# GLA half chunks laid between the MLA attention blocks, and rotated keys on 128 rows, in a two-layer streaming encoder step

## The chip, the cores and the metric

One Trainium2 chip, one of its cores. The metric is the device time of one execution in microseconds (us), from the program's start to its end. The kernel computes everything in one launch. All arithmetic of the parts below is in float32; a float32 matmul stands in the trace as two records.

## The reference, cut to what matters

The step has two layers on 304 new rows: 16 meta tokens and 256 prompt tokens (group i), and 32 sample tokens (group ii) with a past of 272 cached rows. Layer 0 mixes by two head groups beside each other, whose outputs are joined and projected; each layer then has a layer norm, a mixture of 64 experts, and a second norm. The change lies within the mixer of layer 0:

```python
lg = log_sigmoid(a @ gla_w_g2 + gla_b_g) / 16
o_gla, s_gla = gla_recurrence(q * 64 ** -0.5, k, v, lg, s0)      # 4 heads, chunks of 64 tokens
o_gla = rms_norm(o_gla, gla_norm_g) * silu(r)
...
def step(s, inp):                                                # one GLA chunk
    b = jnp.cumsum(gc, axis=2)
    o_inter = einsum('bhtd,bhdv->bhtv', qc * exp(b), s)          # what the state gives
    att = einsum('bhtd,bhsd,bhtsd->bhts', qc, kc, decay)
    o = o_inter + einsum('bhts,bhsv->bhtv', att, vc)
    s = exp(b_last)[..., None] * s + einsum('bhsd,bhsv->bhdv', kc * exp(b_last - b), vc)
    return s, o
...
s = (einsum('bhqc,bkc->bhqk', q_lat, k_lat) + einsum('bhqr,bkr->bhqk', q_rope, k_rope)) * MLA_SCALE
p = softmax(where(k_chunk <= q_chunk, s, NEG_INF))               # 8 heads
o_lat = einsum('bhqk,bkc->bhqc', p, k_lat)
...
out = concatenate([o_gla, o_mla], axis=-1) @ w_out0
```

A GLA chunk needs the state that the chunk before left. MLA and GLA don't depend on each other until the output projection.

## The kernel before, in words

Tokens lie in three tiles of 128, 128 and 64 columns (the last holds 16 prompt tokens, 32 sample tokens and zeros between). Five engines run programs of their own and wait on semaphores. PSUM has eight banks, and `Banks` gives them out in one fixed order: `bank_uses()` lists every use of a bank in the order in which TensorE issues it, use number i takes bank i modulo 8, `open` makes TensorE wait until the use eight places earlier has been emptied, `full` makes a reader wait for its filling, `copied` waits for a particular use's emptying. So the list sets not only what comes when, but also who waits for whom.

After the input projections and the transposes (until about 102 us) the mixer goes through these stages:

- **Level products** (`level_products(t)`, L1005). For tile t and each of four heads, the causal products within a chunk, by six levels and the diagonal, as small 64-row matmuls into one bank ("att", t, h). VectorE masks the bank (L1621) and sums the levels (L1625) into `att`, in `sum_levels(t)`.
- **Absorbed queries** ("ql", h, L1032): one matmul for each of eight MLA heads; **rotated queries** ("qrT", i, L749): 24 transposes. ScalarE copies both out (L1261).
- **GLA chunks** (`chunk_out(c)`). There are six: four of 64 prompt tokens, one of the last 16 (number 4) and the sample's 32 (number 5). Each has two halves j of two heads. A half takes two banks: ("o", c, j) with the queries on the state (L1018) and the level sums on the values (L1022), which ScalarE copies to `og` (L1261), and ("u", c, j), keys on values (L1025), which VectorE adds to the decayed state in two operations (L1637, `update_state`). A chunk of the prompt waits until the state of the one before has been added.
- The order before was, tile by tile: level products, then absorbed or rotated queries, then the tile's chunks, by `CHUNKS_BY_TILE = [[0], [1], [5, 2, 3, 4]]`. Behind them VectorE made the sums of squares of `og` (L1490, L1652), ScalarE the reciprocal root (L1269, L1270), and the norm (`norm_out`, L1490) was laid into attention steps 1, 3 and 5 on VectorE.
- **Attention** (19 blocks, `attention_blocks()`): for each of eight heads a block of queries 0 to 127 on 144 keys and one of queries 128 to 255 on 272 keys, so even blocks have 144 keys and odd ones 272; block 16 has the 16 tail queries of all heads on 272 keys, and 17 and 18 the sample's queries of four heads each on 320 keys (L765 with `skv_t`, `skr_t`). TensorE's step i issues the scores of block i (latent keys on 128 rows, then rotated keys on 32 rows, L765), the transposes of the probabilities of block i-2 (L749) and the weighted sum of block i-3 (L765, 128-key pieces, the last one 16 or 64 keys). VectorE's step m normalises block m (L1684, L1493), then does the mask, maximum and negation of scores m+2 (L1670, L1672, L1493) and copies the sum of block m-2 (L1497). ScalarE's step m has the exponential of block m+1 (L1375) and the copies of the transposes of block m (L1385, L1386).
- Then the transposes of `og` (L749), the value matmuls of MLA ("om", L1101) and the output projection (L765, 64 records).

SP issues the load of the output weights (4 MB) when the last level product has filled its bank (L639), and the shared expert's weights when the norm is done (L552, L555). POOL stores the GLA states when the last state additions are done (L713).

## Time and profile before

| | us |
|---|---|
| time, median of 3 runs (lowest, highest) | 1508.03 (1506.62, 1508.96) |
| the profiled execution: its time | 1507.37 |
| the profiled execution: its span, first to last instruction | 1505.6 |
| mean granted TensorE clock | 0.942 |
| TensorE busy (PE) | 1435.9, 95% of the span |
| VectorE busy (DVE) | 634.3, 42% |
| ScalarE busy (ACT) | 348.5, 23% |
| first level product | 102.05 |
| first score matmul's load | 159.42 |
| output projection starts | 249.28 |

Two lines of the page's second part show the span in 40 slices of 37.6 us; PE is TensorE's busy share and PEclk its granted clock, in tenths:

```profile
PE   6999899899999999999999978999999999999994
PEclk9996557899999999999999989999999999999997
```

The fourth to the seventh slice (113 to 263 us) are those with a granted clock of 6, 5, 5 and 7 tenths. A granted clock of 1.00 is TensorE's 2.4 GHz level, 0.50 its 1.2 GHz level. The chain of work that ended last lies to 93% on TensorE. In the rows below PE is a matmul, PEld a weight load; a line's last bracket is the engine's idle time before it and who ended it, and "issue" stands for time in which it waited for nothing that the profile shows. A matmul's duration contains its way through the array, so the distance of two starts tells what one costs.

### The profile page before, as it was taken

The numbers are of one execution on the slowest core, as the hardware profiler recorded it, in microseconds if no ns is written. First come the engines' busy times: TensorE is split into PE (matmuls) and PEld (weight loads), VectorE is DVE, ScalarE is ACT, GpSimd is POOL, SyncE is SP. The second block draws the span as 40 slices with busy tenths as digits, with TensorE's granted clock in tenths as the row PEclk, the third lists the DMA queues.
The fourth block names the chain that finished last, engine by engine and source line by source line (L and its number), as shares of the span: only waits on it lengthen the run. The fifth ranks groups of instructions, "written<-read, shape, count | busy, mean of one in ns | idle before, by whom it ended". The sixth has DMA issues, their size and how long they took to land.

```text
span 1505.6 us, 17800 instructions
## 1 busy us (share of the span) xinstructions
PE 1435.9 (95%) x6519; PEld 753.0 (50%) x6519; DVE 634.3 (42%) x1267; ACT 348.5 (23%) x722; POOL 49.1 (3%) x77
## 2 busy tenths in 40 slices
PE   6999899899999999999999978999999999999994
PEld 4565465464454454455445465545445445444542
DVE  0554542562433343344334368334334333433436
ACT  1441321221221222122122213122212122222211
POOL 5200100100000000000000020000000000000000
PEclk9996557899999999999999989999999999999997
DMA  9102020176998999899899842599989989998970
GB/s 297 62 6 113 8 91 0 65 300 270 375 391 349 410 387 393 366 394 392 347 412 391 349 151 103 205 372 391 390 364 395 392 348 410 390 390 364 395 305 31
DMA packets 63623, 435.21 MB, mean 289 GB/s; under 512 B 4324, under 2 KB 6436, under 8 KB 13537
## 3 DMA queue, kind: packets, MB, share of 16 engines
q1 hardware_dynamic: 60800, 427.08, 71.0%
q0 software_dynamic: 2784, 7.62, 1.6%
q8 instruction: 24, 0.39, 0.1%
q14 instruction: 15, 0.12, 0.0%
HBM read 432.93 MB, written 1.76 MB: 289 GB/s over the span
## 4 chain that ended last, share of the span: by engine, by line
PE 93%; DVE 4%; issue 1%; ACT 1%; DMA 0%; SPq 0%; DVEq 0%
PE bank L849 30%; PE bank L765 25%; PE bank L797 15%; PE bank L791 12%; PE bank L749 4%; PE bank L859 1%; PE bank L919 1%; DVE sb_x L1519 1%; PE bank L1025 1%; PE bank L906 1%; DVE sb_x L1515 1%; PE bank L1022 1%; DVE sb_ln_st L1511 1%; PE bank L1018 1%; DMA sb_x<-in_x_sample_dram 0%
## 5 line engine op out<-in xcount | busy, mean ns | idle before, releaser
L1448 DVE TENSOR_TENSOR sb_x<-sb_x,bank 128x512 f32<-128x512 f32 (+1 forms) x396 | 242.0, 678 | 118.7 <-PE bank L791 118.7
L797 PE MATMUL bank<-sb_wslot,sb_ht 128*64 128x512 f32 x1024 | 231.0, 593 | 0.0
L849 PE MATMUL bank<-sb_wslot,sb_xg_own 128*64 128x512 f32 x1024 | 226.5, 595 | 1.7 <-ACT sb_xg_own L1216 1.7
L849 PE MATMUL bank<-sb_wslot,sb_xt 128*64 128x512 f32 x1024 | 226.8, 595 | 0.0
L1467 DVE TENSOR_TENSOR sb_hh<-sb_sg,bank 128x256 f32<-128x256 f32 x64 | 27.0, 421 | 376.8 <-ACT sb_sg L1240 376.8
L1454 DVE SCALAR_TENSOR_TENSOR sb_yl<-bank,sb_gslot,sb_yh 128x512 fp32r<-128x512 f32 x128 | 96.0, 750 | 162.8 <-ACT sb_yh L1222 162.8
L765 PE MATMUL bank<-sb_pick,sb_xh 128*128 128x512 f32 x432 | 160.8, 401 | 0.9 <-DVE sb_x L1817 0.9
L791 PE MATMUL bank<-sb_yh,sb_place 128*128 128x512 f32 x396 | 157.6, 398 | 3.3 <-DVE sb_yl L1454 3.3
L791 PE MATMUL bank<-sb_yl,sb_place 128*128 128x512 f32 x396 | 156.6, 395 | 0.0
L1240 ACT ACTIVATE sb_sg<-bank 128x256 f32<-128x256 f32 x64 | 24.6, 384 | 550.1 <-PE bank L849 550.1
L797 PEld LDWEIGHTS bank<-sb_wslot,sb_ht 128*64 128x64 f32 x1024 | 72.8, 137 | 144.6 <-issue 139.3
L849 PEld LDWEIGHTS bank<-sb_wslot,sb_xg_own 128*64 128x64 f32 x1024 | 71.4, 137 | 140.6 <-issue 139.6
L849 PEld LDWEIGHTS bank<-sb_wslot,sb_xt 128*64 128x64 f32 x1024 | 70.7, 137 | 139.5 <-issue 139.5
L1222 ACT ACTIVATE sb_yh<-bank,sb_gslot 128x512 fp32r<-128x512 f32 x128 | 88.1, 688 | 174.2 <-PE bank L797 174.2
L765 PE MATMUL bank<-sb_pick,sb_xl 128*128 128x512 f32 x288 | 113.7, 395 | 0.0
L765 PEld LDWEIGHTS bank<-sb_pick,sb_xh 128*128 128x128 f32 x432 | 81.3, 188 | 19.1 <-issue 2.6
L791 PEld LDWEIGHTS bank<-sb_yh,sb_place 128*128 128x128 f32 x396 | 74.3, 188 | 27.3 <-DVE sb_x L1448 5.7
L791 PEld LDWEIGHTS bank<-sb_yl,sb_place 128*128 128x128 f32 x396 | 74.5, 188 | 17.1
L1216 ACT ACTIVATE sb_xg_own<-bank 128x512 f32<-128x512 f32 x80 | 47.9, 598 | 79.1 <-PE bank L765 79.1
L765 PEld LDWEIGHTS bank<-sb_pick,sb_xl 128*128 128x128 f32 x288 | 54.3, 188 | 10.1
L1216 ACT ACTIVATE sb_xt<-bank 128x512 f32<-128x512 f32 x64 | 38.3, 599 | 37.7 <-PE bank L765 37.7
L749 PEld LDWEIGHTS bank<-sb_cst,sb_hh 128*128 128x128 f32 x128 | 20.7, 205 | 46.0 <-issue 45.4
(297 smaller groups left out, 1201.1 us busy)
## 6 DMA issues: line engine op xcount, KB each, us to landing
sb_wslot<-in_moe_w_gate_dram SPq DMA_DIRECT2D x64, 2048.0 KB, 8.4
sb_wslot<-in_moe_w_up_dram SPq DMA_DIRECT2D x64, 2048.0 KB, 13.1
sb_wslot<-in_moe_w_down_dram SPq DMA_DIRECT2D x64, 2048.0 KB, 15.3
sb_w_in_hi<-in_w_in_dram SPq DMA_DIRECT2D x2, 2048.0 KB, 24.2
sb_w_in_lo<-in_w_out_dram SPq DMA_DIRECT2D x1, 4096.0 KB, 13.5
sb_w_in_lo<-in_w_in_dram SPq DMA_DIRECT2D x2, 1024.0 KB, 10.3
sb_ln_g<-in_ln_g_dram POOLq DMA_DIRECT2D x4, 512.0 KB, 4.5
sb_ln_b<-in_ln_b_dram POOLq DMA_DIRECT2D x4, 512.0 KB, 6.0
```

The source lines that it names most:

```text
L749: return pe.transpose(dst, src, ident[0:n, 0:n])
L765: last = pe.matmul(dst, lhs, rhs, start=i == 0, stop=i == len(pairs) - 1)
L791: last = pe.matmul(banks.tile[order[f]][:, :], place[u][:, t * P:(t + 1) * P], part[:, c * 512:(c + 1) * 512], start=h == 0, stop=h == 1)
L797: last = pe.matmul(y_b[c][64 * e:64 * e + 64, :], ht[:, k, 64 * e:64 * e + 64], w_down[u][:, e, k * D + c * 512:k * D + (c + 1) * 512], st ...
L849: last = pe.matmul(gu_b[64 * e:64 * e + 64, :], xgt[b][:, k, sl], w_gu[u][:, :, e, k * FE:(k + 1) * FE], start=k == 0, stop=k == DK_SLICES ...
L859: last = pe.matmul(place_b[:, t * PLACED:(t + 1) * PLACED], pick[b][:, t, q * P:(q + 1) * P], spread[:, b, t, :], start=True, stop=True)
L1216: act.activation(xgt[b][:, kk, :], banks.tile[2 + c][:, :], ACT.Copy).then_inc(s[f"xg_copied{c}"], 1)
L1222: act.activation(yh[:, c * 512:(c + 1) * 512], banks.tile[4 + c][:, :], ACT.Copy, scale=gslot[:, u, :]).then_inc(s[f"yh_ready{c}"], 1)
L1240: act.activation(sg[:, :], gu_b[:, 0:FE], ACT.Silu).then_inc(s["sg_ready"], 1)
L1448: dve.tensor_tensor(dst, dst, banks.tile[order[f]][0:rows, :], ALU.add).then_inc(s["added"], 1)
L1454: dve.scalar_tensor_tensor(out=yl[:, cc], in0=banks.tile[4 + c][:, :], scalar=gslot[:, u, :], in1=yh[:, cc].bitcast(F32), op0=ALU.mult, op ...
L1467: dve.tensor_tensor(hh[:, :], sg[:, :], gu_b[:, FE:2 * FE], ALU.mult).then_inc(s["h_ready"], 1)
```

## The change

- `bank_uses()` and TensorE: level products of tiles 0 and 1, absorbed queries, level products of tile 2 and rotated queries now come first. The twelve half chunks (`CHUNK_PARTS`: chunk 0 halves 0 and 1, chunk 1, ... chunk 5) follow one each behind the scores, transposes and weighted sum of attention steps 0 to 11. A half chunk waits only for the state of its own half.
- VectorE: level sums of all tiles first; the state addition of part m at the end of attention step m; squares of tile 0, 1, 2 at the end of steps 6, 10, 13; norm of tile 0, 1, 2 at the end of steps 16, 17, 18.
- ScalarE: the copy of output part m between the exponential of block m+1 and the transposes' copies of block m; the reciprocal root in step 15.
- `kr_t` and `skr_t` get 128 rows, of which rows 32 to 127 are zero (one more memset on POOL), and the score matmul of the rotated keys runs over all 128 rows, with whatever finite numbers lie in the other rows of the query tiles.

The diff, cut to its core:

```diff
-CHUNKS_BY_TILE = [[0], [1], [5, 2, 3, 4]]
+CHUNK_PARTS = [(c, j) for c in range(len(CHUNKS)) for j in range(2)]
+SQUARES_AT = (6, 10, 13)
+ROOT_AT, NORM_AT = 15, (16, 17, 18)
...
+    u += [("att", t, h) for t in range(2) for h in range(GH)] + [("ql", h) for h in range(MH)]
+    u += [("att", 2, h) for h in range(GH)] + [("qrT", i) for i in range(5)]
     n = len(attention_blocks())
     for i in range(n + 3):
         u += [("s", i)] if i < n else []
         u += [("pt", i - 2)] if 0 <= i - 2 < n else []
         u += [("ol", i - 3)] if 0 <= i - 3 < n else []
+        u += [("o",) + CHUNK_PARTS[i], ("u",) + CHUNK_PARTS[i]] if i < len(CHUNK_PARTS) else []
...
-        kr_t = mb("kr_t", [ROPE, T_COLS])
+        kr_t = mb("kr_t", [P, T_COLS])
-        skr_t = mb("skr_t", [ROPE, S_KEYS])
+        skr_t = mb("skr_t", [P, S_KEYS])
...
+            gp.memset(kr_t[:, :], 0.0).then_inc(zeroed, 1)
...
-            def chunk_out(c):
+            def chunk_out(c, j):
                 if 0 < c < 5:
-                    for j in range(2):
-                        banks.copied(pe, ("u", c - 1, j))
+                    banks.copied(pe, ("u", c - 1, j))
...
-            for t in range(TILES):
-                level_products(t)
-                if t < 2:
-                    (absorbed_queries, rotated_queries)[t]()
-                for c in CHUNKS_BY_TILE[t]:
-                    chunk_out(c)
+            level_products(0)
+            level_products(1)
+            absorbed_queries()
+            level_products(2)
+            rotated_queries()
...
-                        ql, qr = q_lat[:, hs[0], q0:q0 + nq], q_rot_t[0:ROPE, hs[0], q0:q0 + nq]
+                        ql, qr = q_lat[:, hs[0], q0:q0 + nq], q_rot_t[:, hs[0], q0:q0 + nq]
...
+                if i < len(CHUNK_PARTS):
+                    chunk_out(*CHUNK_PARTS[i])
...
             for m in range(len(blocks)):
                 if m + 1 < len(blocks):
                     exp_block(m + 1)
+                if m < len(CHUNK_PARTS):
+                    c, j = CHUNK_PARTS[m]
+                    tc, pb, n = CHUNKS[c]
+                    copy(og[pb:pb + n, tc, j * 256:(j + 1) * 256], ("o", c, j), lambda ps: ps[pb:pb + n, 0:256])
+                if m == ROOT_AT:
+                    act.wait_ge(gss_ready, TILES)
+                    rsqrt(grs[:, :], gss[:, :], 1.0 / GDV, eps[:, 1:2], grs_ready)
...
                     scores(m + 2)
                 if m >= 2:
                     latent_out(m - 2)
-                if m == 0:
+                if m < len(CHUNK_PARTS):
+                    update_state(*CHUNK_PARTS[m])
+                if m in SQUARES_AT:
+                    square_sums(SQUARES_AT.index(m))
+                if m == NORM_AT[0]:
                     dve.wait_ge(grs_ready, 1)
-                if m in (1, 3, 5):
-                    norm_out(m // 2)
+                if m in NORM_AT:
+                    norm_out(NORM_AT.index(m))
```

## Rows read from the trace of the kernel before

**Rows 1.** Stretches: busy time (instructions) by engine, granted clock, DMA share, GB/s.
```profile
105.00:111.00 6.00, 4.37 (x20) 2.11 (x18) 5.50 (x7) 2.88 (x8) 0.00 (x0) 1.00 0.01 3
...
121.60:124.70 3.10, 3.10 (x17) 2.20 (x16) 3.00 (x4) 1.52 (x3) 0.00 (x0) 0.50 0.00 0
...
136.00:158.00 22.00, 20.13 (x51) 8.64 (x52) 4.73 (x14) 2.63 (x7) 0.00 (x0) 0.50 0.30 122
172.00:235.00 63.00, 63.00 (x174) 38.57 (x174) 28.32 (x97) 14.68 (x60) 0.00 (x0) 0.50 0.14 55
...
248.00:276.00 28.00, 27.07 (x67) 11.92 (x64) 7.19 (x11) 0.29 (x1) 0.00 (x0) 1.00 0.00 1
```

**Rows 2.** Timeline: rotated-query transposes, and the first score load: start us, us, engine.
```profile
121.58 4.05 PE L749 MATMUL bank<-sb_cst,sb_q_rot 128*32 128x128 f32 x24
...
159.42 0.50 PEld L765 LDWEIGHTS bank<-sb_kv_t,sb_w_in_hi 128*128 128x128 f32 x2 [1.42 <-issue]
```

**Rows 3.** Timeline of two attention steps, weight loads: start us, us, engine, line, what.
```profile
208.13 0.50 PEld L765 LDWEIGHTS bank<-sb_kv_t,sb_w_in_hi 128*128 128x128 f32 x2 [0.22 <-issue]
...
209.34 0.50 PEld L765 LDWEIGHTS bank<-sb_kr_t,sb_w_in_hi 32*128 32x128 f32 x2 [0.70 <-issue]
...
210.54 0.41 PEld L749 LDWEIGHTS bank<-sb_cst,sb_w_in_hi 128*128 128x128 f32 x3 [0.70 <-issue]
...
211.03 0.55 PEld L765 LDWEIGHTS bank<-sb_w_in_hi,sb_ckv_n 128*128 128x128 f32 x2
...
212.52 0.50 PEld L765 LDWEIGHTS bank<-sb_kv_t,sb_w_in_hi 128*128 128x128 f32 x2 [0.23 <-issue]
...
214.07 0.20 PEld L749 LDWEIGHTS bank<-sb_cst,sb_w_in_hi 128*128 128x128 f32 x2 [0.28 <-issue]
...
214.34 0.98 PEld L765 LDWEIGHTS bank<-sb_w_in_hi,sb_ckv_n 128*128 128x128 f32 x4
...
216.27 0.50 PEld L765 LDWEIGHTS bank<-sb_kv_t,sb_w_in_hi 128*128 128x128 f32 x2 [0.22 <-issue]
```

**Rows 4.** Timeline: transposes of block 17, and the output projection.
```profile
235.09 0.45 PEld L749 LDWEIGHTS bank<-sb_cst,sb_w_in_hi 128*128 128x128 f32 x3 [0.22 <-DVE sb_w_in_hi L1493]
...
249.28 27.70 PE L765 MATMUL bank<-sb_w_in_lo,sb_xt 128*128 128x512 f32 x64 [0.94 <-DVE sb_xt L1497]
```

**Rows 5.** Timeline of VectorE's level masks, tile 0 and tile 2.
```profile
104.28 0.62 DVE L1621 TENSOR_TENSOR sb_att_m<-bank,sb_mix 128x448 f32<-128x448 f32 x1
...
105.89 0.62 DVE L1621 TENSOR_TENSOR sb_att_m<-bank,sb_mix 128x448 f32<-128x448 f32 x1
...
131.51 0.61 DVE L1621 TENSOR_TENSOR sb_att_m<-bank,sb_mix 16x80 f32<-16x80 f32 x2
...
132.96 0.61 DVE L1621 TENSOR_TENSOR sb_att_m<-bank,sb_mix 16x80 f32<-16x80 f32 x2
```

**Rows 6.** Timeline of GLA half chunks at either clock, with a state addition.
```profile
125.55 0.19 PEld L1018 LDWEIGHTS bank<-sb_s_p,sb_qe_t 128*64 128x64 f32 x2
...
127.33 0.19 PEld L1018 LDWEIGHTS bank<-sb_s_p,sb_qe_t 128*64 128x64 f32 x2 [0.33 <-issue]
...
137.60 0.29 PEld L1018 LDWEIGHTS bank<-sb_s_p,sb_qe_t 128*64 128x64 f32 x2 [0.65 <-issue]
...
140.84 0.29 PEld L1018 LDWEIGHTS bank<-sb_s_p,sb_qe_t 128*64 128x64 f32 x2 [0.65 <-issue]
...
144.25 0.73 DVE L1637 SCALAR_TENSOR_TENSOR sb_s_p<-sb_s_p,sb_u_t,bank 64x128 f32<-64x128 f32 x2 [2.50 <-PE bank L1025]
145.05 0.29 PEld L1018 LDWEIGHTS bank<-sb_s_p,sb_qe_t 128*64 128x64 f32 x2 [1.63 <-issue]
```

**Rows 7.** Timeline of the steps of rows 3, VectorE: reciprocal behind the scores' three operations and copy.
```profile
212.09 0.15 DVE L1684 RECIPROCAL sb_stat<-sb_stat 128x1 f32<-128x1 f32 x1
...
215.36 0.15 DVE L1684 RECIPROCAL sb_stat<-sb_stat 128x1 f32<-128x1 f32 x1
```

**Rows 8.** Timeline: one of the norm's two operations on VectorE.
```profile
180.27 0.69 DVE L1490 TENSOR_TENSOR sb_og<-sb_og,sb_g_gla 128x512 f32<-128x512 f32 x1
```

More of the change, by code:

```diff
@@ L1013, in chunk_out @@
                 if 0 < c < 5:
[L1014 to L1027 removed]
+                    banks.copied(pe, ("u", c - 1, j))
+                ps = banks.open(pe, ("o", c, j))
+                pe.matmul(ps[pb:pb + n, 0:256], qe_t[:, j, c0:c0 + n], st[:, j, :], start=True, stop=False)
+                for b in range(2):
+                    h = 2 * j + b
+                    pe.wait_ge(att_ready, 4 * t + h + 1)
+                    last = pe.matmul(ps[pb:pb + n, b * P:(b + 1) * P], att[pb:pb + n, t, h, o0:o0 + n],
+                                     v_sb[pb:pb + n, t, h * P:(h + 1) * P], start=False, stop=b == 1)
+                last.then_inc(banks.fill_sem(("o", c, j)), 1)
+                stage(("u", c, j), lambda ps: pe.matmul(ps[:, 0:256], kd[pb:pb + n, t, j * P:(j + 1) * P],
+                                                        v_sb[pb:pb + n, t, j * 256:(j + 1) * 256],
+                                                        start=True, stop=True))
             def absorbed_queries():
@@ L1323, in _ @@
                 act.activation(kv_t[:, cols], ps[:, 256:256 + rows], ACT.Copy)
-                act.activation(kr_t[:, cols], ps[0:ROPE, 384:384 + rows], ACT.Copy).then_inc(banks.empty_sem(n), 1)
+                act.activation(kr_t[0:ROPE, cols], ps[0:ROPE, 384:384 + rows], ACT.Copy).then_inc(banks.empty_sem(n), 1)
             for g in range(TILES):
@@ L1328, in _ @@
                 act.activation(skv_t[:, g * P:g * P + rows], ps[:, 0:rows], ACT.Copy)
-                act.activation(skr_t[:, g * P:g * P + rows], ps[0:ROPE, P:P + rows], ACT.Copy).then_inc(banks.empty_sem(n), 1)
+                act.activation(skr_t[0:ROPE, g * P:g * P + rows], ps[0:ROPE, P:P + rows], ACT.Copy).then_inc(banks.empty_sem(n), 1)
             copy(uk_t[:, :, :], ("ukT",), lambda ps: ps[:, :].rearrange("p (g n) -> p g n", g=4))
@@ L1363, in _ @@
                 banks.copied(act, ("qrT", i))
-            for src, dst in ((q_lat, q_few), (q_rot_t[0:ROPE, :, :], q_few_rot)):
+            for src, dst in ((q_lat, q_few), (q_rot_t[0:ROPE, :, :], q_few_rot[0:ROPE, :])):
                 for c0, q0, nq in ((0, 2 * P, TAIL), (MH * TAIL, SAMPLE0, N_DEC)):
@@ L1626, in sum_levels, with update_state @@
                              att_ready if i + 1 == len(parts_) else None)
-            def update_state(c):
+            def update_state(c, j):
                 t, pb, n = CHUNKS[c]
                 st = s_s if c == 5 else s_p
-                for j in range(2):
-                    name = ("u", c, j)
-                    ps = banks.full(dve, name)
-                    last = t * P + pb + n - 1
-                    for b in range(2):
-                        hp, hc = slice(64 * b, 64 * b + 64), slice(128 * b, 128 * b + 128)
-                        ins = dve.scalar_tensor_tensor(out=st[hp, j, hc], in0=st[hp, j, hc], scalar=u_t[hp, j, last:last + 1],
-                                                       in1=ps[hp, hc], op0=ALU.mult, op1=ALU.add)
-                        step.banked(ins, banks, name) if b else step(ins)
+                name = ("u", c, j)
+                ps = banks.full(dve, name)
+                last = t * P + pb + n - 1
+                for b in range(2):
+                    hp, hc = slice(64 * b, 64 * b + 64), slice(128 * b, 128 * b + 128)
+                    ins = dve.scalar_tensor_tensor(out=st[hp, j, hc], in0=st[hp, j, hc], scalar=u_t[hp, j, last:last + 1],
+                                                   in1=ps[hp, hc], op0=ALU.mult, op1=ALU.add)
+                    step.banked(ins, banks, name) if b else step(ins)
             dve.wait_ge(state_in, 16 * GH)
@@ L1643, in _, with square_sums @@
                 sum_levels(t)
-                for c in CHUNKS_BY_TILE[t]:
-                    update_state(c)
-            for c in range(len(CHUNKS)):
-                for j in range(2):
+            def square_sums(t):
+                rows = ROWS[t]
+                for c, j in CHUNK_PARTS[4 * t:4 * t + 4]:
                     banks.copied(dve, ("o", c, j))
-            for t in range(TILES):
-                rows = ROWS[t]
                 tt(sq[0:rows, :], og[0:rows, t, :], og[0:rows, t, :], ALU.mult)
```

49 lines of the change are left out of this document (10 added, 39 removed).

## The prediction

> **What bounds the kernel now.** I read the page first. Its line of the granted clock is near full for most of the span and about half in the slices that follow the input projections. Then I cut that part into stretches [rows 1]: from 172 to 235 us TensorE has no idle time in the profile (63.00 us of 63.00) and yet the granted clock is 0.50, so its 1.2 GHz level. This is the MLA attention. From 136 to 158 us, the GLA chunks, it is also 0.50, with 20.1 of 22 us busy. So the stage in question (102 to 249 us) is bound by TensorE at the lower of its two levels, and by a chain through VectorE in front of that. Everything behind 249.3 us (output projection, the two MoE layers) is not touched; I take it as 1507.4 - 249.3 = 1258 us that shifts as a whole. The sum is made against the profiled execution, 1507.4 us (span 1505.6); the median of the runs is 1508.0, 0.7 us more.
>
> What the clock did: it fell after 105 to 111 us, where TensorE was busy 4.4 of 6 us and mostly with 64-row matmuls in single pieces, and a second time after the waits of tile 2's level sums. It rose at the end of the only stretch in between in which 128-row instructions ran end to end (the 24 rotated-query transposes from 121.58 us [rows 2]) and again in the 128-row output matmuls, before 248 us. In the attention, where half of the score matmuls have 32 rows, it never rose between 172 and 235 us [rows 1].
>
> **The change part by part.**
>
> *128 rows for the rotated keys.* In the trace a matmul whose row count differs from the one before it starts late: the weight load of the rotated keys begins only 1.20 us after that of the latent keys, and the next transposes 1.20 us after that [rows 3]. Price of the columns alone: the output projection has 64 records, two to a 512-column matmul, in 27.70 us at full clock, 0.866 us a matmul [rows 4], 1.69 ns a column, so 3.38 ns at half clock. A 272-column matmul is 0.92 us and not 1.20; a 144-column one 0.49 and not 0.78. If both halves have the same rows, and only the first load (0.16 us) is open, the score block costs 2.00 instead of 2.40 us and 1.13 instead of 1.55. That is 0.4 us in each of 19 blocks, 8 us at half clock.
>
> The Trainium skill ("TensorE: Matmul & The Clock Gate", Why this matters for your kernels) speaks against this part: it gives a single matmul with 32 rows the same time as one with 128, so more rows would buy nothing. The trace doesn't settle it, as no such matmul of 128 rows is in it; it shows an open load at each change of rows, and I go by that. By the page the sum would be 8 us more (rival 4).
>
> *Level products of all tiles ahead.* VectorE's sums become one run: 8 heads at 1.61 us from 104.28 (105.89 - 104.28) and 4 at 1.45 (132.96 - 131.51) [rows 5], over at 123 us. The banks go round in the order of the list, so the last absorbed query waits for the eighth sum's first half: 104.28 + 7 x 1.61 + 0.6 = 116.2. Behind it: that matmul 1.3, tile 2's level products 1.6, the transposes 4.3 (4.05 in the trace, partly at full clock) and copies of the last query part and of the few-token queries 2.2 [rows 2]. First score at 125.6 us, 33.8 earlier than 159.42.
>
> *GLA half chunks between the blocks.* One costs TensorE 3.24 us at half clock (140.84 - 137.60) and 1.78 at full (127.33 - 125.55) [rows 6]. Twelve of them, 38.9 us, are work that is moved, not removed; what the laying between should hide is the wait for the state (145.05 against 140.84 + 3.24 = 144.08 without it, 1.0 us). **But it adds a longer wait.** With five banks taken in each block the output bank of block i-3 is the one that the state product of half chunk i-2 held. VectorE empties that only in its step i-2, and there it stands behind the mask, maximum and negation of score block i and a latent copy. So in each of blocks 4 to 12, TensorE does scores, transposes, and then waits before the weighted sum; behind the waiting instruction are queued that sum, the next half chunk and the next scores. The chunk's own wait, for the state of half chunk i-2, binds in the same way in blocks 2 and 3. Length: from the last score column to the reciprocal behind the copy, 212.09 - 210.41 = 1.68 us (210.41 is the start of the transposes' load, 210.54, less 0.13 of open load), plus two state additions 0.73 and 0.07 to the waiting load [rows 6, 7]: 2.48 us; for the 144-column block 215.36 - 213.94 + 0.80 = 2.22.
>
> *The sum at half clock*, load to load. A block's weighted sum, from its first load to the next scores: 216.27 - 214.34 = 1.93 with three key tiles, 212.52 - 211.03 = 1.49 with two [rows 3].
> Blocks 0 and 1: 1.13 + 3.24 and 2.00 + 3.24: 9.6. Blocks 2 and 3, with the chunk's wait: 6.3 + 7.4 = 13.7. Blocks 4 to 11: even 1.13 + 2.22 + 1.93 + 3.24 = 8.5, odd 2.00 + 2.48 + 1.49 + 3.24 = 9.2, four pairs less 0.6 for the short parts: 70.2. Block 12: 5.2. Blocks 13 to 15, as before but 0.4 less each: 11.3. Blocks 16 to 18: 13.2. Then a wait of 1.4, since the norm of tile 0 (two operations of 0.69 [rows 8]) now stands on VectorE in front of the probabilities of block 17. The tail from block 17's transposes to the output projection, 249.28 - 235.09 = 14.2 [rows 4]. Together 138.8; the projection starts at 264.4 instead of 249.3: **+15.1 us**.
>
> *What is hidden.* The squares (1.4 us of VectorE each, at blocks 6, 10, 13) lie behind a state addition, where VectorE has some 4 us until the next scores. The root's two table loads (1.28 us each) lie in block 15 on ScalarE, idle about 2 us a block at half clock, and its result is wanted a block later; at full clock they would cost up to 2 us. The stores of the states, the 4 MB load of the output weights (now issued some 11 us earlier) and the shared expert's loads, issued later, all land before their readers. The added memset on POOL is 0.4 us in front of a wait of 8.9. Cost nothing.
>
> *What the clock gives back.* Blocks 13 and on are now 128-row work without waits and nearly without open loads (in a 320-column block 2.2 us of scores, 0.6 of transposes and 0.9 of sums in one piece): the kind of stretch after which the clock rose at 125 and 248 us. I expect it to rise between blocks 13 and 17. By 1.78 against 3.24, and with VectorE's latency in the way, I take 38% off what is left: of 38.8 us from block 13 that is 15, of 23.3 from block 17 that is 9. I take 12. In blocks 4 to 12 TensorE stands still for about 2 us in each 9 (5 to 6 at full clock), as in the stretches after which it fell; a rise there is given back.
>
> Forecast: 1507.4 + 15.1 - 12 = **1510.5 us**, its own range 1505 to 1515.
>
> **The rivals.**
> 1. *The clock is up for much of the interleaved blocks.* For it: a 272-column score pair with transposes and a 128-row half chunk beside it is over 2.5 us of unbroken 128-row work; against it: the waits. If it were up from the first block on, a pair takes 4.7 of waits and 0.55 x 13.0 of TensorE's work, 11.9 instead of 17.7 us, so 23 us less in blocks 4 to 11, and at 38% 8 before and 16 behind: -47, 1475.5. Up for half of the interleaved blocks and all of the rest: 1491. Chance 0.28, over 1475 to 1498.
> 2. *The bank wait does not bind* (VectorE is through before TensorE comes to the sum). Then each of blocks 4 to 12 loses the wait less the transposes, about 1.8 us: 16 less, and the clock as forecast: 1494. Against it: VectorE's operations are in a fixed order and the scores stand first. Chance 0.10.
> 3. *Slower: the clock stays at its lower level to the end of the attention*, as before. It decides if even the 320-column blocks don't raise it: 1522.5. Chance 0.12.
> 4. *The 128 rows buy no time*: a change of operand keeps its load open whatever the rows, at 0.4 us in each of 19 blocks 8 us more, 1518. (The page named above would have it so.) Against it: between transposes and sums, all of 128 rows, no load is open. Chance 0.08.
> The forecast has 0.42.
>
> **How the numbers follow.** The predicted time is the forecast's. Range: 1477 to 1522 leaves out the end of rival 1 (0.07) and about half of rival 3. A measurement of this kernel tells 0.2%, 3 us, from no change: 1505 to 1511. Faster: rivals 1 and 2, and 0.03 of the forecast, 0.41. Slower: rivals 3 and 4 and 0.12 of the forecast, 0.32. Same: 0.27. The likeliest case is close to no change because two large terms, 39 us moved in and 34 us of earlier start, nearly cancel.
>
> **What would show it.** First score load at about 125.6 us; the rotated-key loads with 128 rows begin within 1.0 us of the latent ones; before the weighted sums of blocks 4 to 12 TensorE idles about 2 us and its releaser is the state addition on VectorE; block pairs of 17.7 us at clock 0.50 up to block 12; the clock rising between there and the end; projection start at 252 to 253 us. Wrong if the clock is at 1.00 for more than one block within the interleaved part (rival 1), or if no releaser from the state additions stands before the sums (rival 2).

## The result, and the profile after

The changed kernel takes 1515.0 us (median of 20 runs, 1508.9 to 1518.1), the kernel before 1507.7 us beside it. The ratio is 1.0045, with a 95% interval of 1.0036 to 1.0053: slower by about 7 us, half a per cent. That is 4.5 us above the forecast of 1510.5, at the upper end of the forecast's own range (1505 to 1515) and within the whole one. The profiled execution took 1515.2 us, with a span of 1513.4. Of the runs below, one of e6's seven ran slower, 1500.3 us at a mean granted clock of 0.943 in place of 0.970, and is not in its ratio. Two lines of the page, TensorE's busy share and its granted clock in 40 slices of 37.8 us:

```profile
PE   6998788999999999999999968999999999999994
PEclk9995558999999999999999998999999999999998
```

The three slices of 5 tenths are the interleaved part. Busy time by stretch (span, TensorE, its weight loads, VectorE, ScalarE, POOL, granted clock, DMA):

```profile
126.40:228.80 102.40, 85.45 (x235) 49.37 (x235) 30.43 (x100) 17.84 (x63) 0.00 (x0) 0.50 0.07 28
228.80:245.90 17.10, 13.05 (x70) 9.27 (x69) 13.92 (x44) 9.39 (x30) 4.32 (x8) 1.00 0.08 17
245.90:256.10 10.20, 9.65 (x38) 6.85 (x39) 5.53 (x12) 2.17 (x5) 0.00 (x0) 0.50 0.62 240
```

Where TensorE had no idle time at all in the attention of before ([rows 1], 63.00 of 63.00 us), it now stands idle for 17 of 102 us, at the lower level of its clock (0.50, 1.2 GHz). Then it is at 1.00 (2.4 GHz) for 17.1 us and falls again. Weight loads of TensorE: the first block; one even block; and the end of the attention up to the output projection at 258.29 us.

```profile
126.52 0.50 PEld L763 LDWEIGHTS bank<-sb_kv_t,sb_w_in_hi 128*128 128x128 f32 x2 [2.25 <-issue]
126.92 0.58 PEld L763 LDWEIGHTS bank<-sb_kr_t,sb_w_in_hi 128*128 128x128 f32 x2
...
167.86 0.50 PEld L763 LDWEIGHTS bank<-sb_kv_t,sb_w_in_hi 128*128 128x128 f32 x2 [0.65 <-issue]
168.26 0.58 PEld L763 LDWEIGHTS bank<-sb_kr_t,sb_w_in_hi 128*128 128x128 f32 x2
168.75 0.38 PEld L747 LDWEIGHTS bank<-sb_cst,sb_w_in_hi 128*128 128x128 f32 x2
171.25 0.93 PEld L763 LDWEIGHTS bank<-sb_w_in_hi,sb_ckv_n 128*128 128x128 f32 x4 [2.12 <-issue]
...
236.45 0.15 PEld L747 LDWEIGHTS bank<-sb_cst,sb_w_in_hi 128*128 128x128 f32 x2 [1.80 <-DVE sb_w_in_hi L1488]
...
244.92 0.28 PEld L747 LDWEIGHTS bank<-sb_cst,sb_w_in_hi 128*128 128x128 f32 x3 [2.05 <-DVE sb_w_in_hi L1488]
...
258.29 0.30 PEld L763 LDWEIGHTS bank<-sb_w_in_lo,sb_xt 128*128 128x128 f32 x2 [1.47 <-issue]
```

The load of the rotated keys follows the latent one after 0.40 us in a block of 144 keys (168.26 - 167.86) and after 0.61 in one of 272 keys, with no idle time in front of it; before, it followed after 1.20 us in a block of 272 keys and had 0.70 of idle time in front [rows 3]. The weighted sum begins 2.12 us after the transposes' load has ended. The view of waits from 100 to 265 us names who ended that idle time (engine, what it wrote, who released it: us in total, times, longest):

```profile
PE bank L763 <- DVE sb_s_p L1631: 13.5, 8, 1.7
...
PE bank L763 <- DVE sb_s_s L1631: 1.7, 1, 1.7
```

L1631 is the state addition. Nine waits, in blocks 4 to 12, 15.2 us: the bank wait of the prediction. The wait of 1.80 us at 236.45, with the clock at 1.00, is another. VectorE's timeline at the end of step 13 and the start of step 14:

```profile
234.27 0.29 DVE L1492 COPY sb_w_in_hi<-bank 128x128 f32<-128x128 f32 x1
234.48 0.67 DVE L1485 TENSOR_TENSOR sb_sq<-sb_og 64x512 f32<-64x512 f32 x1
235.19 0.68 DVE L1644 TENSOR_REDUCE sb_gss<-sb_sq 64x4 f32<-64x512 f32 x1
235.90 0.16 DVE L1676 RECIPROCAL sb_stat<-sb_stat 128x1 f32<-128x1 f32 x1
236.10 0.29 DVE L1488 TENSOR_SCALAR sb_w_in_hi<-sb_w_in_hi,sb_stat 128x144 f32<-128x144 f32 x1
```

The squares of tile 2, 1.42 us from start to the reciprocal, stand in front of the probabilities (236.10) for which TensorE waits. The 2.05 us at 244.92, in front of the transposes of block 17, are those behind the norm of tile 0.

### The profile page after: what moved, and what is told of

It reads as the page before. It is cut to its first block, busy times and chain, and to the rows that moved or that the text cites. A ratio compares the mean times of both kernels' runs of the same rounds, so it can differ in the third digit from the quotient of the medians.

```text
span 1513.4 us, 17808 instructions
## 1 busy us (share of the span) xinstructions
PE 1426.2 (94%) x6519; PEld 748.4 (49%) x6519; DVE 634.7 (42%) x1267; ACT 350.2 (23%) x723; POOL 49.6 (3%) x78
## 4 chain that ended last, share of the span: by engine, by line
PE 91%; DVE 6%; issue 1%; ACT 1%; DMA 1%; SPq 0%; DVEq 0%; ACTq 0%
PE bank L847 30%; PE bank L763 24%; PE bank L795 15%; PE bank L789 12%; PE bank L747 3%; PE bank L857 1%; PE bank L917 1%; PE bank L1021 1%; PE bank L1014 1%; PE bank L1018 1%; PE bank L904 1%; DVE sb_x L1514 1%; PE bank L1161 1%; DVE sb_x L1510 1%; DVE sb_ln_st L1506 1%
## 5 line engine op out<-in xcount | busy, mean ns | idle before, releaser
L789 PEld LDWEIGHTS bank<-sb_yh,sb_place 128*128 128x128 f32 x396 | 74.3, 188 | 27.3 <-DVE sb_x L1443 5.8
## 6 DMA issues: line engine op xcount, KB each, us to landing
sb_w_in_lo<-in_w_out_dram SPq DMA_DIRECT2D x1, 4096.0 KB, 13.8
```

Of the source, the lines that this page charges most:

```text
L789: last = pe.matmul(banks.tile[order[f]][:, :], place[u][:, t * P:(t + 1) * P], part[:, c * 512:(c + 1) * 512], start=h == 0, stop=h == 1)
```

## The experiments

All times are medians, each beside runs of the kernel before on the same chip, which is not the same one for all lines. The medians of the kernel before were 1506.2 to 1507.7 us, so the chips move a comparison of two lines by up to 1.5 us; a line's own uncertainty is in the interval of its ratio, up to 4 us to either side. A trace is one execution: that of e3 lies 4.6 us below its median, that of e4 3.9 below, those of e12 and e6 4.3 and 6.4 above, the others within 3. An *open load* is below a weight load that has idle time in front of it though nothing in the profile holds it up.

| run | rotated keys | order of the work | us | ratio (95%) |
|---|---|---|---|---|
| before | 32 rows | before | 1507.7 | 1 |
| e7 | 64 rows | before | 1507.7 | 0.9998 (0.9985 to 1.0010) |
| e1 | 128 rows | before | 1480.3 | 0.9829 (0.9811 to 0.9847) |
| e2 | 32 rows | changed | 1529.3 | 1.0146 (1.0129 to 1.0164) |
| after | 128 rows | changed | 1515.0 | 1.0045 (1.0036 to 1.0053) |
| e4 | 128 rows | changed, norm at steps 12 to 14 | 1517.3 | 1.0072 (1.0054 to 1.0090) |
| e11 | 128 rows | changed, norm left out | 1507.3 | 1.0004 (0.9987 to 1.0021) |
| e5 | 32 rows | changed, addition first | 1511.8 | 1.0026 (1.0013 to 1.0039) |
| e3 | 128 rows | changed, addition first | 1470.4 | 0.9747 (0.9719 to 0.9775) |
| e6 | 128 rows | as e3, norm spread | 1467.4 | 0.9729 (0.9712 to 0.9747) |
| e8 | 128 rows, sums too | as e3 | 1459.5 | 0.9689 (0.9665 to 0.9714) |
| e9 | 128 rows, sums too | before | 1472.7 | 0.9781 (0.9756 to 0.9806) |
| e10 | 128 rows | levels ahead, no half chunk between blocks | 1466.3 | 0.9734 (0.9711 to 0.9757) |
| e12 | 128 rows, sums too | as e10, squares, root and norm earlier | 1456.3 | 0.9670 (0.9646 to 0.9694) |

### The two halves of the change apart: e1 and e2

e1 is the kernel before with the diff's lines on `kr_t`, `skr_t`, `q_few_rot` and the score matmul alone:

```diff
-        kr_t = mb("kr_t", [ROPE, T_COLS])
+        kr_t = mb("kr_t", [P, T_COLS])
...
-                        ql, qr = q_lat[:, hs[0], q0:q0 + nq], q_rot_t[0:ROPE, hs[0], q0:q0 + nq]
+                        ql, qr = q_lat[:, hs[0], q0:q0 + nq], q_rot_t[:, hs[0], q0:q0 + nq]
```

> The kernel before with nothing but the rotated keys on 128 rows; order of the work as before. Step of the prediction (each block saves the open weight load of the rotated queries, 0.42 us in 19 blocks at granted clock 0.50): 1507.7 - 8 = 1499.7 us, and the clock stays at 0.50 from about 136 to 245 us. Rival 4 (rows buy nothing): 1507.7 us within 0.2%. Rival 1 (the fuller blocks bring the clock up within the attention): a stretch of several blocks at 1.00 between 160 and 235 us, under 1493 us.

Measured: 1480.3 us, 27 us less. My step said 8. The last of the three ways holds (rival 1), at 13 us less than the bound that I gave it. Two stretches of e1, columns as above:

```profile
172.00:187.00 15.00, 14.38 (x45) 10.66 (x46) 8.46 (x27) 3.51 (x15) 0.00 (x0) 0.50 0.00 1
195.00:212.00 17.00, 16.01 (x91) 12.20 (x91) 11.76 (x43) 7.42 (x29) 0.00 (x0) 1.00 0.23 98
```

And from its timeline, the weight loads with which blocks 6 to 8 and 10 to 12 begin, and the transposes of block 6's step:

```profile
180.23 0.50 PEld L766 LDWEIGHTS bank<-sb_kv_t,sb_w_in_hi 128*128 128x128 f32 x2 [0.23 <-issue]
180.64 0.58 PEld L766 LDWEIGHTS bank<-sb_kr_t,sb_w_in_hi 128*128 128x128 f32 x2
181.98 0.20 PEld L750 LDWEIGHTS bank<-sb_cst,sb_w_in_hi 128*128 128x128 f32 x2 [0.77 <-DVE sb_w_in_hi L1494]
...
184.18 0.50 PEld L766 LDWEIGHTS bank<-sb_kv_t,sb_w_in_hi 128*128 128x128 f32 x2 [0.22 <-issue]
...
188.02 0.30 PEld L766 LDWEIGHTS bank<-sb_kv_t,sb_w_in_hi 128*128 128x128 f32 x2 [0.17 <-issue]
...
194.72 0.30 PEld L766 LDWEIGHTS bank<-sb_kv_t,sb_w_in_hi 128*128 128x128 f32 x2 [0.22 <-issue]
...
196.49 0.30 PEld L766 LDWEIGHTS bank<-sb_kv_t,sb_w_in_hi 128*128 128x128 f32 x2
...
198.56 0.30 PEld L766 LDWEIGHTS bank<-sb_kv_t,sb_w_in_hi 128*128 128x128 f32 x2
```

Block 7 takes 184.18 to 188.02, 3.84 us; block 13, also of 272 keys, was 4.39 before (208.13 to 212.52 [rows 3]), so an odd block gains 0.55. In an even block TensorE now waits 0.77 us for VectorE's probabilities before the transposes, and a pair from block 6 on (180.23 to 188.02) costs 7.79 against 8.14 (208.13 to 216.27 [rows 3]): 0.35 a pair, and not 0.8. The direct saving is thus even smaller than I said. The rest is the clock: the trace has it at 1.00 from 194.7 us to beyond the end of the attention, with blocks 10 and 11 at 1.77 and 2.07 us. The row count is all that was changed, and it brought the clock up within the attention.

e2 is the other half, the reordering alone: the changed kernel with the diff of e1 undone.

> The changed kernel with the rotated keys on 32 rows again. If the rows save 0.42 us a block also where a block waits for the state addition (that wait runs from the end of the scores, so the saving is not swallowed): 1515.0 + 8 = 1523 us, block pairs of about 18.5 us in place of 17.67. If the state addition's wait swallows it: 1515. If the rise of the clock at 228.8 us hangs on the padded blocks too, it comes later or not at all and the time is 1527 or more.

Measured: 1529.3 us; the third way. In its trace the first level product is 2.2 us earlier than in that of the changed kernel (101.19 against 103.34), yet the clock rises only at 263.7 us, not at 228.8. So the reordering alone costs 21.7 us, and the rows take 14.3 of them back.

### The wait: e3 and e5

```diff
-                if m + 2 < len(blocks):
-                    scores(m + 2)
-                if m >= 2:
-                    latent_out(m - 2)
                 if m < len(CHUNK_PARTS):
                     update_state(*CHUNK_PARTS[m])
+                if m + 2 < len(blocks):
+                    scores(m + 2)
+                if m >= 2:
+                    latent_out(m - 2)
```

> The changed kernel with one line moved: in its step m VectorE adds the state of half chunk m before the scores of block m+2, not last. The bank that the weighted sum of block i-3 takes is then empty before the scores of block i are even read. Theory (TensorE's 1.8 us idle ahead of the sums of blocks 4 to 11, 2.12 and 2.18 us in two of them less about 0.4 that any sum has, is this wait and nothing behind it is late): 8 to 9 blocks x 1.8 = 14 to 16 us less, 1499 to 1501 us, block pairs of about 14.1 us, clock still 0.50 there. Rival (another wait takes its place: scores m+2 come 1 us later on VectorE, so the exponentials and the transposes' wait move instead): 1510 to 1515 us with a new releaser before the transposes. Rival (with the idle time gone the clock rises in the interleaved blocks): 1475 to 1490 us.

Measured: 1470.4 us, 44.6 less than the changed kernel. In the interleaved blocks the wait is gone and no other took its place. The waits were 15 us; the other 30 came with the clock (the last of the three ways, and 5 us beyond it). Timeline of e3, weight loads from block 6 to block 8:

```profile
149.77 0.30 PEld L763 LDWEIGHTS bank<-sb_kv_t,sb_w_in_hi 128*128 128x128 f32 x2 [0.33 <-issue]
150.00 0.31 PEld L763 LDWEIGHTS bank<-sb_kr_t,sb_w_in_hi 128*128 128x128 f32 x2
150.25 0.21 PEld L747 LDWEIGHTS bank<-sb_cst,sb_w_in_hi 128*128 128x128 f32 x2
150.48 0.94 PEld L763 LDWEIGHTS bank<-sb_w_in_hi,sb_ckv_n 128*128 128x128 f32 x6
...
153.31 0.30 PEld L763 LDWEIGHTS bank<-sb_kv_t,sb_w_in_hi 128*128 128x128 f32 x2 [0.33 <-issue]
...
157.17 0.19 PEld L763 LDWEIGHTS bank<-sb_kv_t,sb_w_in_hi 128*128 128x128 f32 x1 [0.33 <-issue]
```

The sum's load follows the transposes' within 0.23 us, and the pair takes 7.40 us (149.77 to 157.17) in place of 17.7. Of the 10.3 us about 3.7 are the wait, by the pairs of the two runs with 32 rows, both at 0.50: 18.26 us with the wait (e2, first two lines) and 14.60 without (e5, last two).

```profile
167.28 0.50 PEld L762 LDWEIGHTS bank<-sb_kv_t,sb_w_in_hi 128*128 128x128 f32 x2 [0.65 <-issue]
...
185.54 0.50 PEld L762 LDWEIGHTS bank<-sb_kv_t,sb_w_in_hi 128*128 128x128 f32 x2 [0.65 <-issue]
```

```profile
162.22 0.50 PEld L762 LDWEIGHTS bank<-sb_kv_t,sb_w_in_hi 128*128 128x128 f32 x2 [0.65 <-issue]
...
176.82 0.50 PEld L762 LDWEIGHTS bank<-sb_kv_t,sb_w_in_hi 128*128 128x128 f32 x2 [0.65 <-issue]
```

The other 6.6 are the same instructions at the other level of the clock, as the stretch of e3 shows:

```profile
142.00:177.00 35.00, 33.92 (x182) 22.04 (x181) 23.76 (x78) 12.72 (x47) 0.00 (x0) 1.00 0.00 1
```

Is the idle time enough of an explanation for the low clock? e5 takes the wait away with 32 rows: the diff of e3 made, that of e1 undone.

> The changed kernel with the state addition ahead of the scores on VectorE (as in the run before this one) and the rotated keys on 32 rows again. Theory A (the idle time ahead of the sums alone held the clock at 0.50): without it the clock rises here too within the first five blocks, and the time is the 1470.4 us of the run with 128 rows and 4 to 8 more, under 1485. Theory B (the clock needs the fuller blocks as well): it stays at 0.50 up to the end of attention as it does with 32 rows and the wait (1529.3); only the wait of 1.5 us in 8 to 9 blocks goes, 12 to 14 us, and the time is 1515 to 1518 us.

Measured: 1511.8 us, 17.5 less than e2: theory B, though 3 us below the time that I gave it. The 17.5 us are the price of the wait with the clock held, over the 12 to 14 that I expected. TensorE is then busy all the time, at 0.50; a stretch of e5:

```profile
142.00:205.00 63.00, 63.00 (x173) 33.90 (x171) 21.82 (x73) 11.57 (x45) 0.00 (x0) 0.50 0.00 0
```

So with either of the two left in, the row-count changes of the rotated keys (e5) or the idle time of the bank wait (the changed kernel), the clock stayed down in the interleaved blocks; with both gone (e3) it rose there and stayed up for 41 us. One trace qualifies this. e11, further below, has the wait and 128 rows, and in it the clock was up for a part of block 4:

```profile
143.80:150.60 6.80, 4.60 (x25) 2.77 (x25) 2.92 (x11) 1.86 (x8) 0.00 (x0) 1.00 0.00 0
```

It fell again there at 150.6 us, so with the wait left in a rise did not last.

### What the rows do: e7

```diff
-        kr_t = mb("kr_t", [ROPE, T_COLS])
+        kr_t = mb("kr_t", [64, T_COLS])
...
-                        ql, qr = q_lat[:, hs[0], q0:q0 + nq], q_rot_t[0:ROPE, hs[0], q0:q0 + nq]
+                        ql, qr = q_lat[:, hs[0], q0:q0 + nq], q_rot_t[0:64, hs[0], q0:q0 + nq]
```

> The kernel before with the rotated keys on 64 rows, not 128 (rows 32 to 63 zero): the row count of the loads still changes twice a block. With 128 rows the kernel before took 1480.3 us. Theory A (the gain is the load that stands open where the row count changes, and what shorter blocks do to the clock): the open load is still there, 1507.7 us within 3. Theory B (the clock answers to how much of the array the rotated keys fill, whatever the loads do): it rises later than with 128 rows but within attention, 1488 to 1502 us. Theory C (the open load goes with 64 rows too): 1480 to 1490 us.

Measured: 1507.7 us, theory A to the microsecond. The weight loads of an odd block look as those of before with 32 rows [rows 3], with the same 0.70 us of idle time on both sides:

```profile
208.65 0.50 PEld L766 LDWEIGHTS bank<-sb_kv_t,sb_w_in_hi 128*128 128x128 f32 x2 [0.22 <-issue]
209.86 0.50 PEld L766 LDWEIGHTS bank<-sb_kr_t,sb_w_in_hi 64*128 64x128 f32 x2 [0.70 <-issue]
211.06 0.41 PEld L750 LDWEIGHTS bank<-sb_cst,sb_w_in_hi 128*128 128x128 f32 x3 [0.70 <-issue]
```

Doubling the rows buys nothing; making them equal to the neighbours' does. The load is open where the row count changes. Whether the clock answers to the open loads or to the rows themselves is not shown: no run has rotated matmuls of 128 rows with their loads open, the two come together here.

### The norm and the second fall: e4, e6, e11

```diff
-SQUARES_AT = (6, 10, 13)
-ROOT_AT, NORM_AT = 15, (16, 17, 18)
+SQUARES_AT = (6, 10, 11)
+ROOT_AT, NORM_AT = 12, (12, 13, 14)
```

> The changed kernel with the last squares at step 11, the reciprocal root at step 12 and the norm of the three tiles at steps 12, 13 and 14 in place of 15 and 16 to 18. Theory (the norm steps stand before the probabilities of blocks 17 and 18 at the full clock, waits of 1.80 and 2.05 us, and the clock falls behind them at 245.9 us): the waits go, 2.5 to 4 us, and without the fall 5 us more come back: 1506 to 1512 us. Rival (the norm delays VectorE as much in steps 12 to 14): 1515 within 0.2%.

Measured: 1517.3 us, no gain, as the rival has it; what stands in the way is the squares more than the norm. In e4's step 11 VectorE has the last state addition and the squares of tile 2 in a row, 227.20 to 229.38, in front of the probabilities, and TensorE waits 2.31 us; the fall moved with the wait. After 226.6 us the clock is at 1.00 for one short stretch in which TensorE is busy for 1.31 of 3.40 us, and then at 0.50 for 10.2 us. The transposes' load in e4, and the two stretches:

```profile
229.93 0.19 PEld L747 LDWEIGHTS bank<-sb_cst,sb_w_in_hi 128*128 128x128 f32 x2 [2.31 <-DVE sb_w_in_hi L1488]
```

```profile
226.60:230.00 3.40, 1.31 (x8) 0.91 (x8) 3.12 (x10) 2.82 (x7) 1.49 (x3) 1.00 0.05 12
230.00:240.20 10.20, 10.20 (x32) 7.43 (x32) 7.71 (x21) 4.20 (x14) 2.73 (x6) 0.50 0.11 25
```

```diff
-                o = og[0:rows, t, :].rearrange("p (h n) -> p h n", h=GH)
-                tt(o, o, bc(grs[0:rows, t * GH:(t + 1) * GH], 2, GDV), ALU.mult)
-                tt(o, o, bc(g_gla[0:rows, :], 1, GH), ALU.mult, og_ready)
+                o = og[0:rows, t, 0:GH]
+                tt(o, o, grs[0:rows, t * GH:(t + 1) * GH], ALU.mult, og_ready)
```

> The changed kernel with the two multiplications of the output norm cut to 4 columns of each tile (the norm is left out of the computation), everything else and all waits as they are. Theory (the norm on VectorE in steps 16 to 18 makes TensorE wait and so lets the clock fall at 245.9 us): the waits of about 2 us before the transposes of blocks 17 and 18 go and the clock stays at 1.00 to the projection: 7 to 9 us less, 1506 to 1508 us. Rival (VectorE's own attention chain is what TensorE waits for there at the full clock, and the fall comes without the norm too): 1511 to 1515 us.

Measured: 1507.3 us, 7.7 less than the changed kernel. That is the theory's time, but not all of it for the theory's reason. From the scores of block 12 to the projection it takes 32.6 us (214.1 to 246.7) where the changed kernel takes 37.9 (220.4 to 258.3): 5.3 us, and the clock stays at 1.00 from 229.1 us on. The rest is not the norm's: in this profile the first level product is 2.5 us earlier, and the clock was at 1.00 from 143.8 to 150.6 us, so the agreement of the total is in part luck. In place of the 2.05 us of after, the wait in front of block 17's transposes is, in e11's timeline,

```profile
238.28 0.28 PEld L747 LDWEIGHTS bank<-sb_cst,sb_w_in_hi 128*128 128x128 f32 x3 [0.80 <-DVE sb_w_in_hi L1488]
```

Spreading the norm over every other step, on top of e3:

```diff
-SQUARES_AT = (6, 10, 13)
-ROOT_AT, NORM_AT = 15, (16, 17, 18)
+SQUARES_AT = (6, 9, 12)
+ROOT_AT, NORM_AT = 13, (14, 16, 18)
```

> State addition ahead of the scores, squares at steps 6, 9 and 12, the root at 13 and the norms at 14, 16 and 18, every other step. In the run with the state addition first TensorE waits for the probabilities 1.51 and 0.97 us behind squares and the last state addition, 2.67 and 1.06 us behind the norms, and the clock falls at 178.8 and at 199.3 us. Theory (a VectorE step with a norm beside it is the excess, so that spread out each norm is taken up by the step behind it): 3 to 10 us less than 1470.4. Rival (at the full clock every step of blocks 12 to 18 is bound by VectorE's chain, so that 1.4 us of norm costs 1.4 us wherever it stands, and a fall of the clock only moves): 1470.4 within 3 us.

Measured: 1467.4 us; its interval and e3's overlap, so theory and rival are not told apart. The fall comes at 176.0 instead of 178.8 us.

### The same open load at the sums: e8 and e9

The last piece of each weighted sum has 16 or 64 rows, and the traces show 0.22 to 0.23 us of idle time in front of its load and as much behind at the lower clock. In the trace of before, inside the block of [rows 3]:

```profile
211.80 0.50 PEld L765 LDWEIGHTS bank<-sb_w_in_hi,sb_ckv_n 16*128 16x128 f32 x2 [0.22 <-issue]
```

Padding it needs zeros in the unused rows of the probabilities and of `ckv_n`. e8 has this edit on top of e3, e9 on top of e1:

```diff
-                        (src[0:rows, k, :], p_t[0:rows, m % 2, k, :]) for k, rows in key_tiles(m)]))
+                        (src[:, k, :], p_t[:, m % 2, k, :]) for k, rows in key_tiles(m)]))
...
+            step(dve.memset(p_t[:, :, 1:TILES, :], 0.0))
             scores(0)
...
+            gp.memset(ckv_n[:, 2, :], 0.0).then_inc(zeroed, 1)
```

> The state addition first (1470.4 us), and the last piece of every weighted sum also on 128 rows: the unused rows of the probabilities zero, in place of a piece of 16 or 64 rows. In the traces so far the piece of 16 rows stands open for 0.23 us at granted clock 0.50 and the score load behind it for 0.22, and at 1.00 no gap shows there. Theory A (it is the same open load as the rotated keys' was): 0.45 us in each block that runs at 0.50, some 9 of the 19 blocks, 4 us, and the clock, which answered to the rotated keys' 0.42 us a block, rises earlier or stays longer: 1452 to 1466 us. Theory B (only the open loads go, the clock keeps its times): 1466. Rival (blocks at the full clock are bound by VectorE's chain and the fall behind block 13 comes as before): within 3 us of 1470.4.

> The kernel before with rotated keys and the last pieces of the sums on 128 rows, order of the work as before. With the rows alone it took 1480.3 us and the clock rose for good at 194.7 us, in block 10. Theory A: 0.45 us less in each of ten blocks at 0.50 (4.5 us) and the clock rises some blocks sooner; a block of about 3.9 us at 0.50 takes 2.2 at 1.00, so 1.7 us for each of 3 to 7 blocks: 1464 to 1471 us. Rival (only the loads): 1476.

Measured: e8 1459.5 us (10.9 less than e3), e9 1472.7 (7.6 less than e1): theory A in e8, between theory A and its rival in e9. At the lower clock e8's sum over two key tiles is one row of four loads, and the next load stands 1.20 us behind its start (first two lines), against 1.49 before (211.03 to 212.52 [rows 3]).

```profile
140.73 0.98 PEld L764 LDWEIGHTS bank<-sb_w_in_hi,sb_ckv_n 128*128 128x128 f32 x4
141.93 0.29 PEld L1015 LDWEIGHTS bank<-sb_s_p,sb_qe_t 128*64 128x64 f32 x2 [0.22 <-issue]
...
144.94 0.75 PEld L764 LDWEIGHTS bank<-sb_w_in_hi,sb_ckv_n 128*128 128x128 f32 x6
145.81 0.19 PEld L1015 LDWEIGHTS bank<-sb_s_p,sb_qe_t 128*64 128x64 f32 x2
```

The padding also saves at the full clock, although no idle time shows there. A sum over three key tiles takes 0.87 us up to the next load in e8 (last two lines), and 1.06 in e3 (150.48 to 151.54). A block pair takes 7.02 us in e8 (151.26 to 158.28) and 7.40 in e3. So part of the 10.9 us is shorter work at the full clock, and part is the clock: it holds from 143.1 to 194.3 in e8, where e3 had it fall at 178.8. In e9 it rises for the rest of the attention at 181.9 us, not at 194.7.

### What laying the half chunks between the blocks is worth: e10 and e12

In e10 all twelve half chunks stand in front of block 0; the copies on ScalarE and the state additions on VectorE move with them.

```diff
             rotated_queries()
+            for part in CHUNK_PARTS:
+                chunk_out(*part)
...
-                if i < len(CHUNK_PARTS):
-                    chunk_out(*CHUNK_PARTS[i])
```

> The changed kernel (with 128 rows), but all twelve half chunks between the rotated queries and block 0, none between the blocks: of the reordering only the level products ahead is left. Reference points: order as before with 128 rows 1480.3, interleaved 1515.0, interleaved with the state addition first 1470.4. Theory A (interleaving makes the whole loss, the level products ahead nothing): 1480 within 4 us. Rival (the level products ahead cost or gain by themselves): outside 1476 to 1484, and how much says which.

Measured: 1466.3 us, 14 less than e1 and not 1480: the rival. What was left of the change is not only the level products ahead, as I had written, but also that a half chunk waits for its own half's state alone, and that the squares, the root and the norm come later. Stretch of the half chunks in e10:

```profile
122.00:142.00 20.00, 20.00 (x99) 9.73 (x96) 8.52 (x25) 5.58 (x14) 0.00 (x0) 1.00 0.47 188
```

The half chunks run in a row, TensorE without idle time and at the full clock but for the last one; before, most of those of tile 2 ran at 0.50, with waits of up to 1.63 us for the state [rows 6]. Beside e3 (1470.4) it shows that laying the half chunks between the attention blocks gains nothing that these runs can tell: the intervals 0.9711 to 0.9757 and 0.9719 to 0.9775 overlap. The gain lies in the rest of the edit; its parts were not run apart.

e12 is e10 with the padded sums of e8 and

```diff
-SQUARES_AT = (6, 10, 13)
-ROOT_AT, NORM_AT = 15, (16, 17, 18)
+SQUARES_AT = (0,)
+ROOT_AT, NORM_AT = 2, (4, 6, 8)
...
+            for i, part in enumerate(CHUNK_PARTS):
+                update_state(*part)
+                if i in (5, 9):
+                    square_sums(i // 4 - 1)
```

> The version with the level products ahead and no half chunk between the blocks (1466.3 us), with the last pieces of the sums on 128 rows as well (two pairs so far: 10.9 and 7.6 us less), the squares of tiles 0 and 1 beside the half chunks where VectorE is busy for 2 of 5 us, those of tile 2 at step 0, the root at step 2 and the norm at steps 4, 6 and 8. Theory (the two gains add, and the waits of 1.80, 2.06 and 1.05 us that stand before the transposes of blocks 14, 17 and 18 go): 1466.3 - 8 - 3 = 1455 us. Rival (the norm costs the same at any step at the full clock): 1458 to 1460. Rival (TensorE can't use the shorter sums since VectorE's chain bounds the blocks at the full clock): 1464 to 1467.

Measured: 1456.3 us, the lowest median, some 50 us under the kernel before. It is where the first theory put it (1455), but its interval (1453 to 1460) holds the first rival's 1458 to 1460 as well. The waits that the theory named shrank and moved: before the transposes of blocks 14, 17 and 18 they are now 0.75, 0.84 and 1.02 us, but with the norm at steps 4, 6 and 8 TensorE waits 1.90, 1.51 and 1.50 us before the transposes of steps 7, 9 and 11, and 1.49 us for ScalarE behind the root. And its interval overlaps e8's, so the order with and without half chunks between the blocks is not told apart here either.

## Why the prediction was right in its sum and short in its size

**First score.** 126.52 us against 125.6. The first level product stood at 103.34 and not 102.08; over the profiles of all these kernels it stood anywhere from 100.4 to 103.4, so I take 1.3 us of this for no effect of the change. Less that, 125.3.

**The sum at the lower clock** held to a few tenths: blocks 0 and 1 took 9.8 us (9.6), 2 and 3 13.8 (13.7), 4 to 11 70.2 (70.2), block 12 5.3 (5.2). A pair is 17.7 us, as said, and the releaser is the state addition. That VectorE's order puts the addition behind the next scores, and the bank list puts the sum on the addition's bank, could be read off the code; its length came from three rows [rows 6, 7]. Rival 2 falls.

**The clock rose** at 228.8 us, in block 13, the early end of "between blocks 13 and 17". **What the clock gives back** is the term that was mis-sized. The cold sum gave 264.4 us for the projection, with the 1.3 us from upstream 265.7; it began at 258.3, so 7.4 us came back and not 12. And 12 lay between 15 for a rise in block 13 and 9 for one in block 17: for the rise that came, my own figure was 15, twice what was measured. The step took 38% off all that was left, with VectorE's latency allowed for in that one figure. It did not have that at the full clock VectorE's chain is what TensorE waits for: I counted one wait of 1.4 us for the norm, and the trace has 2.05, and behind it the clock fell for 10.2 us. e11 prices the norm and this fall at 5.3 us. The squares failed in the same way: "lie behind a state addition, where VectorE has some 4 us" held for tiles 0 and 1 at 0.50, but those of tile 2 stand in step 13, where there is no addition any more and the clock had risen, and cost up to their 1.4 us. e4 shows that its earlier steps don't help, with the squares then in step 11. "At full clock they would cost up to 2 us" stood in the prediction for the root's table loads but wasn't carried into the sum. The remaining 1.2 us, in our favour, lie behind the projection. Together, profile against profile: 15.1 + 1.3 - 7.4 - 1.2 = 7.8 us slower, where 15.1 - 12 = 3.1 was forecast.

**The 128 rows.** "0.4 us in each of 19 blocks" was right as to the cause (e7) and wrong as to where its worth lies. At the lower clock a pair gains 0.35 us in e1, since VectorE is then late in the even blocks. In the changed kernel it was worth 14.3 us, in the order of before 27.3, beside the addition first 41.4: nearly all of it is clock. Rival 4 falls: 128 rows against 32 gave 27 us. The Trainium skill ("TensorE: Matmul & The Clock Gate", Why this matters for your kernels) has one matmul of 32 rows take as long as one of 128. It speaks of a single matmul. For 32 against 64 rows e7 agrees, 1507.7 us both; in the stream between neighbours of 128 rows e1 took 27 us less with 128, as a load of equal row count shows no idle time in front and that of another does. The same page (Step-by-step: what each phase is for) has weight loads pulled ahead if the row groups don't conflict or the load goes to the background buffer; here the loads of 128 rows behind 128 rows, whose row groups are the same, show no idle time.

**Rival 1** did not come to pass in the changed kernel: 102 us at 0.50. "Against it: the waits" was the right reason: e3 shows that without them the clock rises. e5 and e2 show a second condition that the prediction did not have, since there the row-count changes kept it down. My price for the rival, 1475 us with the clock up throughout, was worked out with the waits still in; the 1470 of e3 has them gone, with the clock up for blocks 3 to 13 and in parts of what follows.

**The sign.** Two terms nearly cancelled, 33.8 us of earlier start and 38.9 us of half chunks moved in, and the wait came on top. e5 has that balance without the wait and with the clock held: 4 us slower than before. What was missed is that "nearly cancels" holds at one clock level only. The direction was not seen either: the chances gave faster 0.41, slower 0.32 and same 0.27, and it came out slower.

**Luck.** The sum came nearer than its parts. By the prediction's terms the rows alone give 1499.7 us, and e1 has 1480.3; the reordering alone gives 1518.5 (8 us above the forecast), and e2 has 1529.3. The two errors, 19 and 11 us, have opposite signs. Nor do the parts add: 27 us less and 22 more would be 5 less, and together they gave 7 more. The whole was 4.5 off.

## What to carry to other kernels

TensorE stood here at its lower level without a gap, and a few tenths a block were worth tens of microseconds. Where a trace looks like that, look for what interrupts the work on 128 rows, a change of the row count or a short wait, and take all of it away, since one left over kept the level low here (e5, and the changed kernel). When work is laid between the steps of a pipeline, list for each buffer of the ring who empties it and where that stands in its engine's program: one addition moved in VectorE's order was worth 45 us here with 128 rows, and 17.5 with 32. And test the parts of a change apart: this one held a gain of 27 us, and beside it a loss of 35, which is 22 with 32 rows.

## What the runs showed of the hardware that I had not expected

- The rotated keys' load has 0.70 us of idle time in front with 32 and with 64 rows, at the lower clock, and none with 128 between loads of 128. At the full clock no idle time shows in e3's row of six loads (150.48 us), which holds a piece of 16 rows, and yet a piece of 128 rows in its place made the row 0.19 us shorter (1.06 and 0.87 us): busy time alone hides the open load.
- The same instructions of an attention pair with two half chunks took 7.4 us at 1.00 and, by an estimate, 14.0 at 0.50 (the 17.7 of the changed kernel less the 3.7 of waits between e2 and e5): a factor of 1.9.
- The clock's level at one place depends on small things: with the same instructions but for the norm, one profile has 1.00 from 143.8 to 150.6 us and the other 0.50 there. Part of the difference between two versions can be of this kind: of the time the intervals hold it, of a single trace nothing does.
